# Expert weights in a decoder block: low parts in place, eight load slots instead of six, four high buffers instead of three, and an index column copied one expert ahead

## The chip, the cores and the metric

The kernel runs on one core of one Trainium2 chip. The metric is the device time of one execution in microseconds. The engines are TensorE (PE, with its weight loads as PEld), VectorE (DVE), ScalarE (ACT), GpSimd (POOL) and SyncE (SP), which here issues most of the DMAs.

## The reference, cut to what matters

One hybrid decoder block on 512 tokens of width 1024, all in float32: a token mixer (Mamba-2 scan and causal pooling), then a mixture of 32 experts of which each token takes four, then an embedding gate and a final norm. The change touches the experts only:

```python
gu = xb @ w_gate_up[e] + b_gate_up[e]          # (rows, 1024) @ (1024, 2048)
gate, up = jnp.split(gu, 2, axis=-1)
gate = jnp.minimum(gate, SWIGLU_LIMIT)
up = jnp.clip(up, -SWIGLU_LIMIT, SWIGLU_LIMIT)
act = (up + 1.0) * gate * jax.nn.sigmoid(SWIGLU_ALPHA * gate)
return act @ w_down[e] + b_down[e]             # (rows, 1024) @ (1024, 1024)
```

The rows of an expert are gathered from the normed tokens, and its results are weighted and added to the residual at the same tokens. An expert has 8 MiB of gate and up weights and 4 MiB of down weights, so the 32 experts read 384 MiB.

## The kernel before

The products are made more exact by splitting each operand in two parts. The high part is what a copy to the type float32r keeps, the low part is the operand minus its high part. A product is then high x high + low x high + high x low, three matmuls for one.

The weights come in chunks of 1 MiB, 128 partitions by 2048 numbers, twelve for an expert (`CHUNKS`): eight of gate and up (`UP`), each 128 input rows by 2048 columns, and four of down (`DN`), each two blocks of 128 by 1024. Every chunk goes the same way. SP loads it into one of the six slots of `ring` (`RING`; lines 696 to 709) as soon as the slot's last content has been subtracted, which it sees by `lo_done`. ACT copies it to one of three buffers `split_h` (`SPLIT`; `high`, line 1298), for which it waits for the load (`e_loaded`) and for PE to have used the chunk three before (`chunk_used`). DVE subtracts the copy from the slot into one of three buffers `split_l` (`low`, line 1924), for which it waits for `hi_done`. PE multiplies with the high part after `hi_done` and with the low part after `lo_done`, and then raises `chunk_used`. So after the subtraction the slot is free, and PE needs the two split buffers only.

The chunks form one sequence over all experts: gate-up chunks of expert e+1 stand before the down chunks of expert e, which PE multiplies while ACT and DVE make the activation of expert e+1. `chunk_at(j, e, i)` gives a chunk's number, counted from the loop body of expert e: i from 0 to 7 are gate-up chunks, 8 to 11 down chunks, and 12 onward the next ones.

The experts are sorted by how many rows they have. The fuller ones take up to 96 rows (`ROWS`), with their rows' high and low parts in two tiles, `xgT_h` and `xgT_l`: three groups of four matmuls for each gate-up chunk. The others take at most 64 rows (`HALF`), and then the high parts of the rows stand in the lower half of the columns of `xgT_h` and their low parts in the upper half: two groups for each chunk (`half_gate_up`, `half_down`), after which the two halves of the sum are joined by way of `fold` or `y_fold` (`join_halves`). The two kinds alternate; the loops of PE, ACT, DVE and POOL step over pairs, those of SP over single experts.

Each engine's order is written out by hand. ACT's list for an expert has, between its twelve `high` copies, the gate's silu (`gate`, or `halves_out` and `half_gate`), the high parts of the next rows turned (`turned_high`, line 1292), the y output scaled out of PSUM (`y_out`, `half_down_out`, `half_y_out`), and the activation turned. DVE's list has, between its twelve `low` subtractions, `up` (line 1912: the clipped up part, and the product with the silu, `act_done`) and the low parts of what was turned (`turned_low`, line 1931).

POOL fetches the rows: for each expert it waits until PE has turned the last fetched rows (`et_done`), copies the column of row numbers of the expert three ahead from the table `slots` to `icur`, and issues an indirect DMA from `h_rows` into `xg` (`gather`, line 910, `fetch`, line 903). Then it waits for the expert's y (`y_evac`), copies its column to `dcur`, and issues an indirect DMA that adds `y_sb` to `x1_rows` (`scatter`, line 931); when this has landed it raises `y_free`, for which ACT waits before it writes `y_sb` or `y_fold` again. It also copies each expert's weights to `wcur`.

SP's order is: four DMAs for the bias of the next expert (they wait for `bias_used`), eight gate-up loads, four down loads; before each load stands one wait. `position` reads an expert's number out of the sorted list.

Of the kernel before, what the change touches and what calls it, by code (L numbers as in the profile page):

```python
# [50 lines left out]
RING = 6  # L51
SPLIT = 3
# [134 lines left out]
def program(nc, x, p, mix_norm_g, w_in, conv_w, conv_b, dt_bias, a_log, d_skip, ssd_norm_g,  # L187
# [4 lines left out]
    with ctx:  # L192
# [172 lines left out]
        ring = [here(f"ring{i}", [P, 2 * DM], F32) for i in range(RING)]  # L365
# [9 lines left out]
        split_l = [here(f"split_l{i}", [P, 2 * DM], F32R) for i in range(SPLIT)]  # L375
# [7 lines left out]
        icur = here("icur", [ROWS, 1], I32)  # L383
        dcur = here("dcur", [ROWS, 1], I32)
# [136 lines left out]
        e_loaded = [sem(f"e_loaded{i}") for i in range(RING)]  # L521
# [66 lines left out]

        def chunk_at(j, e, i):

            return j * NE * CHUNKS + e * CHUNKS + UP + i

        def raw_loaded(j, e, i):

            return (j * (NE * CHUNKS // RING) + e * (CHUNKS // RING) + (UP + i) // RING + 1) * 16

# [15 lines left out]
        def _(sp):  # L612
# [91 lines left out]
            def down(j, e, i, of, r):  # L704

                slot = (UP + i) % RING
                sp.wait_ge(lo_done, chunk_at(j, e, i) + 1)
# [11 lines left out]
            def weights(j, ahead=0):  # L719
# [10 lines left out]
                with sp.Fori(1 if ahead else 0, NE - 1) as e:  # L730
                    of, after = (position(sp, e), position(sp, e + 1)) if ahead else (e, e + 1)
                    bias_parts(j * NE + e + 1, after)
                    for k in range(UP):
                        gate_up(j, e, k, after, k)
                    for r in range(DN):
                        down(j, e, UP + r, of, r)
                of = position(sp, NE - 1) if ahead else NE - 1
# [12 lines left out]
            for k in range(RING):  # L750
                gate_up(0, 0, k - UP, 0, k, True)
# [11 lines left out]
            for k in range(RING, UP):  # L763
                gate_up(0, 0, k - UP, 0, k)
# [28 lines left out]
        def _(pool):  # L793
# [109 lines left out]
            def fetch(rows=ROWS):  # L903

                g.indirect_dma_start(out=xg[0:rows, :], out_offset=None, in_=h_rows,  # L905
                                     in_offset=bass.IndirectOffsetOnAxis(ap=icur[0:rows, 0:1], axis=0),
# [24 lines left out]
            def scatter(n, col, steps, following=None, landed=True, rows=ROWS):  # L931
# [16 lines left out]
            def one_pass(j):  # L948
# [36 lines left out]

                if isinstance(j, int):
                    rows_of(0, ROWS, ROWS)
                    with pool.Fori(0, PAIRS - 1) as i:
                        rows_of(i * 2 + 1, HALF, ROWS)
                        rows_of(i * 2 + 2, ROWS, HALF)  # L990
# [34 lines left out]
        def _(act):  # L1025
# [272 lines left out]
            def high(j, e, i):  # L1298

                at, s = chunk_at(j, e, i), UP + i  # L1300
                act.wait_ge(e_loaded[s % RING], raw_loaded(j, e, i))
                act.wait_ge(chunk_used, at + CHUNKS - SPLIT + 1)
                a.activation(split_h[s % SPLIT][:, :], ring[s % RING][:, :], ACT.Copy).then_inc(hi_done, 1)  # L1303
# [44 lines left out]
            def one_pass(j):  # L1348
# [40 lines left out]
                def rest(e, more, rows_in, rows_act, folds=None):  # L1389

                    turned_high(t0 + 3 + e * 2, xgT_h, rows_in, 1.0 if more else 1.0 / ALPHA)
                    for i in range(12, 14):
                        high(j, e, i)
                    if folds is not None:
                        half_down_out(e, e)
                    high(j, e, 14)
                    if folds is None:
                        y_out(j, e, 11, n0 + e)
                    else:
                        half_y_out(e, folds)  # L1400
                    high(j, e, 15)
                    if more:
                        turned_high(t0 + 4 + e * 2, actT_h, rows_act, 1.0 / ALPHA)
                        for i in range(16, 22):
# [1335 lines left out]
```

## Time and profile before

| | us |
|---|---|
| median of 3 runs | 1766.81 |
| lowest and highest | 1766.56, 1767.76 |
| the profiled execution | 1766.66 |
| its span | 1764.9 |

Granted clock of TensorE in that execution: 0.998 of full speed. Busy in the span: PE 1698.8 us (96%), DVE 1381.7 (78%), ACT 1200.8 (68%), POOL 713.1 (40%).

The span is the time from the first to the last instruction of the profiled execution. Engines are shown by how long they worked on instructions; waiting isn't counted. "DMA share" is the mean busy share of the 16 DMA engines, by the time their packets took, and it can pass 1 a little since packets overlap. In an instruction row the bracket tells how long the engine sat idle before it and what ended the wait. "DMA to landing" is the time from issue to the completion of a load. Busy shares of a whole run mix two stages here: the projections and the scan up to about 650 us, the experts from there to about 1690.

### The profile page before, as it was taken

The page shows a single profiled execution, that of the slowest core. Times are in us where ns is not written, and L with a number is a line of the kernel's source. Part 1 is how long each engine was busy: PE and PEld are TensorE (multiplying, and loading weights), DVE is VectorE, ACT ScalarE, POOL GpSimd, SP SyncE. Part 2 cuts the span into 40 slices and gives each one's busy share as a digit, 9 for nine tenths or more (in the row PEclk, how much of TensorE's full clock was granted, in tenths as well). Part 3 has the DMA queues.
Part 4 walks back from the last instruction along what each step waited for, and adds up shares of the span by engine and source line. Part 5 has one row for each costly group of instructions (what it writes and reads, how often), then busy time and mean ns, then how long its engine had stood idle before and what let it go on. Part 6 is the DMA issues. An engine that isn't in the chain of part 4 may idle for free.

```text
span 1764.9 us, 24895 instructions
## 1 busy us (share of the span) xinstructions
PE 1698.8 (96%) x8477; PEld 1346.8 (76%) x8477; DVE 1381.7 (78%) x1048; ACT 1200.8 (68%) x967; POOL 713.1 (40%) x344
## 2 busy tenths in 40 slices
PE   6999999999999999999999999999999999999998
PEld 5878889777888987767767767767767767767776
DVE  4666776755334389999999999999999999999984
ACT  5565555433223368788788788788788788788775
POOL 6124233550000072355465365365365365365110
PEclk9999999999999999999999999999999999999999
DMA  5443343433336469999999999999999999999951
GB/s 177 122 129 85 121 122 107 121 108 119 96 96 231 164 218 397 391 404 392 399 402 392 399 401 392 402 406 388 404 404 391 405 400 398 402 400 395 408 201 49
DMA packets 150865, 504.64 MB, mean 286 GB/s; under 512 B 12733, under 2 KB 73285, under 8 KB 117173
## 3 DMA queue, kind: packets, MB, share of 16 engines
q1 hardware_dynamic: 141652, 478.49, 70.0%
q0 software_dynamic: 9104, 25.28, 6.0%
q8 instruction: 39, 0.64, 0.1%
q14 instruction: 22, 0.17, 0.0%
q10 hardware_dynamic: 48, 0.07, 0.0%
HBM read 487.63 MB, written 20.28 MB: 288 GB/s over the span
## 4 chain that ended last, share of the span: by engine, by line
PE 68%; DVE 14%; issue 9%; ACT 6%; POOL 2%; DVEq 0%; ACTq 0%; POOLq 0%
PE gu_ps L2395 13%; DVE split_l L1928 9%; PE gu_ps L2147 8%; PE gu_ps L2149 8%; PE gu_ps L2148 8%; PE dn_ps L2453 7%; PE gu_ps L2399 7%; PE dn_ps L2459 3%; ACT split_h L1303 3%; PE gu_ps L2409 2%; PE dn_ps L2652 1%; PE gu_ps L2652 1%; PE et_ps L2381 1%; DVE up_sb L1915 1%; PE gu_ps L2169 1%
## 5 line engine op out<-in xcount | busy, mean ns | idle before, releaser
L1928 DVE TENSOR_TENSOR split_l<-ring,split_h 128x2048 fp32r<-128x2048 f32 x384 | 864.8, 2285 | 71.0 <-ACT split_h L1303 69.3
L1303 ACT ACTIVATE split_h<-ring 128x2048 fp32r<-128x2048 f32 x384 | 729.9, 1913 | 113.8 <-PE gu_ps L2399 62.7
L914 POOL COPY icur<-slots 96x1 int32 x30 | 282.8, 9428 | 412.3 <-PE et_ps L2381 410.1
L1536 DVE TENSOR_TENSOR w_lo<-w_raw,w_hi 128x2048 fp32r<-128x2048 f32 (+1 forms) x45 | 104.3, 2318 | 128.8 <-ACT w_hi L1035 122.6
L2409 PE MATMUL gu_ps<-split_l,xgT_h 128*128 128x512 f32 x480 | 139.6, 412 | 17.8 <-DVE split_l L1928 14.0
L2147 PE MATMUL gu_ps<-hT_h,w_hi 128*128 128x512 f32 x392 | 154.6, 394 | 0.6 <-DVE acc L1589 0.6
L2149 PE MATMUL gu_ps<-hT_h,w_lo 128*128 128x512 f32 x392 | 152.7, 390 | 0.0
L2148 PE MATMUL gu_ps<-hT_l,w_hi 128*128 128x512 f32 x392 | 152.6, 389 | 0.0
L2395 PE MATMUL gu_ps<-split_h,xgT_h 128*128 128x512 f32 x512 | 140.6, 396 | 0.9 <-DVE xgT_l L1934 0.9
L2399 PE MATMUL gu_ps<-split_l,xgT_h 128*128 128x512 f32 x512 | 137.2, 390 | 0.0
L2395 PE MATMUL gu_ps<-split_h,xgT_l 128*128 128x512 f32 x512 | 137.2, 390 | 0.0
L2409 PE MATMUL gu_ps<-split_h,xgT_h 128*128 128x512 f32 x480 | 134.4, 402 | 0.0
L2409 PEld LDWEIGHTS gu_ps<-split_l,xgT_h 128*128 128x128 f32 x480 | 83.2, 188 | 64.2 <-DVE split_l L1928 50.7
L1035 ACT ACTIVATE w_hi<-w_raw 128x2048 fp32r<-128x2048 f32 (+1 forms) x45 | 85.0, 1889 | 56.8 <-PE gu_ps L2149 51.4
L923 POOL DMA_INDIRECT slot_rows<-routed,row_idx x16 | 28.2, 1763 | 232.8 <-DVE row_idx L1849 228.3
L2399 PEld LDWEIGHTS gu_ps<-split_l,xgT_h 128*128 128x128 f32 x512 | 96.1, 188 | 20.6
L2395 PEld LDWEIGHTS gu_ps<-split_h,xgT_l 128*128 128x128 f32 x512 | 96.1, 188 | 20.5
L2395 PEld LDWEIGHTS gu_ps<-split_h,xgT_h 128*128 128x128 f32 x512 | 93.7, 188 | 22.3 <-issue 3.4
L2409 PEld LDWEIGHTS gu_ps<-split_h,xgT_h 128*128 128x128 f32 x480 | 86.7, 188 | 26.4 <-issue 9.2
L938 POOL DMA_INDIRECT x_rows<-y_sb,dcur x31 | 91.2, 2942 | 27.6 <-POOL dcur L935 27.6
L905 POOL DMA_INDIRECT xg<-h_rows,icur x31 | 79.8, 2573 | 26.6 <-POOL icur L914 26.3
L2147 PEld LDWEIGHTS gu_ps<-hT_h,w_hi 128*128 128x128 f32 x392 | 73.6, 188 | 16.8 <-issue 1.6
(426 smaller groups left out, 3242.1 us busy)
## 6 DMA issues: line engine op xcount, KB each, us to landing
ring<-in_w_gate_up SPq DMA_DIRECT2D x256, 1024.0 KB, 8.0
ring<-in_w_down SPq DMA_DIRECT2D x128, 1024.0 KB, 9.2
w_raw<-in_w_in SPq DMA_DIRECT2D x28, 1024.0 KB, 5.9
arow<-acum_rows POOLq DMA_DIRECT2D x16, 512.0 KB, 6.5
w_raw<-in_w_ssd_out SPq DMA_DIRECT2D x8, 1024.0 KB, 5.4
w_raw<-in_w_in SPq DMA_DIRECT2D x9, 512.0 KB, 6.1
w_raw<-in_w_mix_out SPq DMA_DIRECT2D x4, 1024.0 KB, 7.9
wpg<-in_w_ple_gate SPq DMA_DIRECT2D x2, 2048.0 KB, 19.9
```

What stands on the lines that cost most here:

```text
L914: g.tensor_copy(icur[:, :], col).then_inc(idx_done, 1)
L938: g.indirect_dma_start(out=x1_rows, out_offset=bass.IndirectOffsetOnAxis(ap=dcur[0:rows, 0:1], axis=0), in_=y_sb[0:rows, :], in_offset=Non ...
L1303: a.activation(split_h[s % SPLIT][:, :], ring[s % RING][:, :], ACT.Copy).then_inc(hi_done, 1)
L1536: v.tensor_tensor(w_lo[RAW_SLOT[n]][:, 0:size], w_raw[RAW_SLOT[n]][:, 0:size], w_hi[HI_SLOT[n]][:, 0:size].bitcast(F32), ALU.subtract).the ...
L1928: v.tensor_tensor(split_l[s % SPLIT][:, :], ring[s % RING][:, :], split_h[s % SPLIT][:, :].bitcast(F32), ALU.subtract).then_inc(lo_done, 1)
L2147: o = t.matmul(pb(key)[:, cols], sh, mh, start=n == 0, stop=False)
L2148: o = t.matmul(pb(key)[:, cols], sh, ml, start=False, stop=False)
L2149: o = t.matmul(pb(key)[:, cols], sl, mh, start=False, stop=n == len(parts) - 1)
L2395: t.matmul(gu_ps[:, b * 512:b * 512 + 512], x[:, k, :], split_h[s][:, b * 512:b * 512 + 512], start=False, stop=False)
L2399: o = t.matmul(gu_ps[:, b * 512:b * 512 + 512], xgT_h[:, k, :], split_l[s][:, b * 512:b * 512 + 512], start=False, stop=k == KD - 1)
L2409: o = t.matmul(gu_ps[:, b * 512:b * 512 + 512], xgT_h[:, k, :], part[s][:, b * 512:b * 512 + 512], start=False, stop=False)
L2453: t.matmul(ps[:, b * 512:b * 512 + 512], x[:, 2 * r + k, :], split_h[s][:, k * DM + b * 512:k * DM + b * 512 + 512], start=r == 0 and k == ...
```

## The change

The low part is written over the slot that it is computed from: `ring_low` are tiles at the addresses of `ring`, and `split_l` is gone. Its three buffers' room goes to two more slots, of the eight that there are now, and to a fourth high buffer. SP may reload a slot when PE has used the chunk in it (`chunk_used`) instead of when it has been subtracted. Since twelve chunks aren't a multiple of eight slots, the loops of SP, ACT, DVE and PE go by pairs of experts, and the slot is found from the place in the pair (`slot_of`). The two new slots use load semaphores that had one use before, hence `before` in `raw_loaded`.

In ACT's list one more `high` stands before the gate, before the turned rows, before the y output and before the turned activation; in DVE's list one more `low` stands before `up`, before the turned rows and before the turned activation.

POOL copies the index column of the rows that it will fetch for the next expert right behind a fetch, into `icur` and `icur_odd` by turns, so that a fetch follows `et_done` at once; and it copies `dcur` before it waits for y.

The diff, cut to its core (the fallback for more than 96 rows, and lines that only hand over the new arguments, are left out):

```diff
-RING = 6
-SPLIT = 3
+RING = 8
+FIRST = 6
+SPLIT = 4
...
-        ring = [here(f"ring{i}", [P, 2 * DM], F32) for i in range(RING)]
+        ring_off = top[0]
+        ring = [here(f"ring{i}", [P, 2 * DM], F32) for i in range(FIRST)]
+        top[0] = ring_off
+        ring_low = [here(f"ring_low{i}", [P, 2 * DM], F32R) for i in range(FIRST)]
...
-        split_l = [here(f"split_l{i}", [P, 2 * DM], F32R) for i in range(SPLIT)]
+        ring_off = top[0]
+        ring += [here(f"ring{i}", [P, 2 * DM], F32) for i in range(FIRST, RING)]
+        top[0] = ring_off
+        ring_low += [here(f"ring_low{i}", [P, 2 * DM], F32R) for i in range(FIRST, RING)]
...
-        e_loaded = [sem(f"e_loaded{i}") for i in range(RING)]
+        e_loaded = [sem(f"e_loaded{i}") for i in range(FIRST)] + yT_loaded[0:RING - FIRST]
...
+        def slot_of(e, i):
+
+            return (in_pair(e)[1] * CHUNKS + UP + i) % RING
...
             def gate_up(j, e, i, of, k, first=False):
 
-                slot = (UP + i) % RING
+                slot = slot_of(e, i)
                 if not first:
-                    sp.wait_ge(lo_done, chunk_at(j, e, i) + 1)
+                    sp.wait_ge(chunk_used, chunk_at(j, e, i) + CHUNKS - RING + 1)
...
-            for k in range(RING, UP):
-                gate_up(0, 0, k - UP, 0, k)
+            for k in range(FIRST, UP):
+                gate_up(0, 0, k - UP, 0, k, True)
...
-                pool.wait_ge(y_evac, n + 2)
-                alone(pool)
-                g.tensor_copy(dcur[:, :], col).then_inc(idx_done, 1)
+                if index_first:
+                    g.tensor_copy(dcur[:, :], col).then_inc(idx_done, 1)
+                pool.wait_ge(y_evac, n + 2)
+                alone(pool)
+                if not index_first:
+                    g.tensor_copy(dcur[:, :], col).then_inc(idx_done, 1)
...
+                def rows_ahead(e, rows_in, rows_out, index, other, more=True):
+
+                    pool.wait_ge(et_done, t0 + e * 2 + 4)
+                    alone(pool)
+                    pool.wait_ge(idx_done, k0 + e * 2 + 4)
+                    alone(pool)
+                    fetch(rows_in, index)
+                    if more:
+                        index_of(e + 4, other)
+                    scatter(e, slots[0:ROWS, column(e), 0], k0 + e * 2 + (6 if more else 5),
+                            slots[0:ROWS, column(e + 1), 1].bitcast(F32), True, rows_out, True)
...
-                act.wait_ge(e_loaded[s % RING], raw_loaded(j, e, i))
+                act.wait_ge(e_loaded[slot_of(e, i)], raw_loaded(j, e, i))
                 act.wait_ge(chunk_used, at + CHUNKS - SPLIT + 1)
...
                 def expert(e, more, rows_in=ROWS, folds=None):
 
-                    gate(j, e, UP - 1, n0 + e + 1)
                     high(j, e, 10)
+                    gate(j, e, UP - 1, n0 + number(e) + 1)
                     high(j, e, 11)
...
                 def half_expert(e, folds):
 
-                    halves_out(e, e + 1)
                     high(j, e, 10)
+                    halves_out(e, number(e) + 1)
+                    high(j, e, 11)
                     half_gate(folds)
-                    high(j, e, 11)
...
-                v.tensor_tensor(split_l[s % SPLIT][:, :], ring[s % RING][:, :], split_h[s % SPLIT][:, :].bitcast(F32),
-                                ALU.subtract).then_inc(lo_done, 1)
+                v.tensor_tensor(ring_low[slot_of(e, i)][:, :], ring[slot_of(e, i)][:, :],
+                                split_h[s % SPLIT][:, :].bitcast(F32), ALU.subtract).then_inc(lo_done, 1)
...
                 def expert(e, more, half_next=False):
 
-                    up(ROWS, chunk_used, chunk_at(j, e, UP - 1) + CHUNKS + 1, n0 + e + 1)
                     low(j, e, 10)
+                    up(ROWS, chunk_used, chunk_at(j, e, UP - 1) + CHUNKS + 1, n0 + number(e) + 1)
                     low(j, e, 11)
```

## Rows read from the trace of the kernel before

**Rows 1.** The page: DMA's busy tenths in 40 slices; the costliest group.

```profile
DMA  5443343433336469999999999999999999999951
...
L1928 DVE TENSOR_TENSOR split_l<-ring,split_h 128x2048 fp32r<-128x2048 f32 x384 | 864.8, 2285 | 71.0 <-ACT split_h L1303 69.3
```

**Rows 2.** The chain that ended last: start us, us, what; two of its pieces.

```profile
1083.61 2.29 DVE split_l L1928
...
1149.40 2.29 DVE split_l L1928
```

**Rows 3.** Busy time by stretch: loads ahead of the experts, clean, after a scatter, one pair.

```profile
core 0: us, PE busy (x) PEld busy (x) DVE busy (x) ACT busy (x) POOL busy (x), PEclk, DMA share, GB/s
570.00:575.00 5.00, 5.00 (x44) 5.00 (x44) 1.91 (x4) 0.00 (x0) 0.00 (x0) 1.00 1.02 431
575.00:580.00 5.00, 5.00 (x45) 5.00 (x44) 0.84 (x2) 2.44 (x4) 0.00 (x0) 1.00 1.01 421
...
1116.45:1119.74 3.29, 3.29 (x16) 2.73 (x15) 3.29 (x3) 2.87 (x2) 3.29 (x1) 1.00 1.03 436
1132.90:1136.19 3.29, 3.29 (x17) 2.71 (x16) 2.86 (x2) 2.49 (x2) 1.15 (x2) 1.00 1.02 354
1136.19:1139.48 3.29, 3.29 (x16) 2.74 (x15) 2.84 (x2) 2.49 (x2) 0.00 (x0) 1.00 1.05 331
1149.10:1214.90 65.80, 63.63 (x292) 47.66 (x292) 61.28 (x33) 54.54 (x35) 35.32 (x11) 1.00 1.02 400
```

**Rows 4.** Timeline of DVE and PE where a half expert begins: start us, us, instruction.

```profile
1142.60 2.29 DVE L1928 TENSOR_TENSOR split_l<-ring,split_h 128x2048 fp32r<-128x2048 f32 x1 [0.43 <-ACT split_h L1303]
...
1144.81 1.22 DVE L1915 TENSOR_SCALAR up_sb<-gu_ps 96x1024 f32<-96x1024 f32 x1
...
1149.54 0.76 PEld L2430 LDWEIGHTS dn_ps<-split_l,actT_h 128*128 128x128 f32 x4 [1.40 <-DVE split_l L1928]
```

**Rows 5.** Waits of the whole run: who for whom, total us, times, longest.

```profile
PEld gu_ps L2409 <- DVE split_l L1928: 50.7, 88, 1.4
...
PEld dn_ps L2430 <- DVE split_l L1928: 28.1, 30, 1.5
...
ACT split_h L1303 <- DMA ring<-in_w_down: 7.3, 11, 1.2
```

**Rows 6.** Weight loads: two single ones by line, then all 24 of a pair.

```profile
L702 SPq DMA_DIRECT2D ring<-in_w_gate_up x1: 332/332/332, 1149.6 to 1149.6; - x1
...
DMA to landing us min/median/max: 6.7/6.7/6.7
...
L702 SPq DMA_DIRECT2D ring<-in_w_gate_up x1: 333/333/333, 1151.8 to 1151.8; - x1
...
DMA to landing us min/median/max: 6.9/6.9/6.9
...
DMA to landing us min/median/max: 6.7/8.9/10.8
```

**Rows 7.** Timeline of DVE in the router: not in place, then in place.

```profile
616.12 0.29 DVE L1816 TENSOR_TENSOR oh<-erow,ixf 128x128 f32<-128x128 f32 x1
...
618.73 0.29 DVE L1860 TENSOR_TENSOR oh<-oh,routed 128x128 f32<-128x128 f32 x1
```

**Rows 8.** Timeline of POOL, and DVE and ACT beside it, in one pair.

```profile
1115.73 9.74 POOL L914 COPY icur<-slots 96x1 int32 x1 [12.39 <-PE et_ps L2381]
...
1118.75 9.08 DVE L1928 TENSOR_TENSOR split_l<-ring,split_h 128x2048 fp32r<-128x2048 f32 x4
...
1129.81 3.24 POOL L938 DMA_INDIRECT x_rows<-y_sb,dcur  x1 [0.90 <-POOL dcur L935]
...
1148.60 10.34 POOL L914 COPY icur<-slots 96x1 int32 x1 [14.54 <-PE et_ps L2381]
...
1153.38 1.02 ACT L1321 ACTIVATE y_fold<-dn_ps 64x1024 fp32r<-64x1024 f32 x1 [0.69 <-PE dn_ps L2419]
...
1159.33 2.29 DVE L1928 TENSOR_TENSOR split_l<-ring,split_h 128x2048 fp32r<-128x2048 f32 x1 [0.44 <-ACT split_h L1303]
```

More of the change, by code:

```diff
@@ L584, in conv_tile, with in_pair, number @@
             return {"X": 4 * g + (key[2] if len(key) > 2 else 0), "B": 16 + g, "C": 20 + g}[key[0]]
+        def in_pair(e):
+            return (0, e) if isinstance(e, int) else e
+        def number(e):
+            return e if isinstance(e, int) else e[0] * 2 + e[1]
         def chunk_at(j, e, i):
-            return j * NE * CHUNKS + e * CHUNKS + UP + i
+            pair, off = in_pair(e)
+            return j * NE * CHUNKS + pair * (2 * CHUNKS) + off * CHUNKS + UP + i
+        def slot_of(e, i):
+            return (in_pair(e)[1] * CHUNKS + UP + i) % RING
         def raw_loaded(j, e, i):
-            return (j * (NE * CHUNKS // RING) + e * (CHUNKS // RING) + (UP + i) // RING + 1) * 16
+            pair, off = in_pair(e)
+            before = 1 if slot_of(e, i) >= FIRST else 0
+            return (j * (NE * CHUNKS // RING) + pair * (2 * CHUNKS // RING) + (off * CHUNKS + UP + i) // RING + 1 + before) * 16
         def passes(eng):
@@ L729, in weights, with expert_loads @@
                     sp.wait_ge(order_done, 1)
-                with sp.Fori(1 if ahead else 0, NE - 1) as e:
-                    of, after = (position(sp, e), position(sp, e + 1)) if ahead else (e, e + 1)
-                    bias_parts(j * NE + e + 1, after)
+                def expert_loads(e):
+                    n = number(e)
+                    of, after = (position(sp, n), position(sp, n + 1)) if ahead else (n, n + 1)
+                    bias_parts(j * NE + n + 1, after)
                     for k in range(UP):
@@ L736, in weights @@
                         down(j, e, UP + r, of, r)
+                with sp.Fori(0, PAIRS) as i:
+                    for off in (1, 2) if ahead else (0, 1):
+                        expert_loads((i, off))
+                if not ahead:
+                    expert_loads(NE - 2)
                 of = position(sp, NE - 1) if ahead else NE - 1
@@ L748, in weights @@
                 alone(sp)
-            for k in range(RING):
+            for k in range(FIRST):
                 gate_up(0, 0, k - UP, 0, k, True)
@@ L2423, in half_down @@
             def half_down(e, r):
-                at, s = chunk_at(0, e, UP + r), (2 * UP + r) % SPLIT
-                for part, ready, count in ((split_h, hi_done, at + 1), (split_l, lo_done, at + RING + 1)):
+                at, high_part, low_part = chunk_at(0, e, UP + r), split_h[(2 * UP + r) % SPLIT], ring_low[slot_of(e, UP + r)]
+                for part, ready, count in ((high_part, hi_done, at + 1), (low_part, lo_done, at + RING + 1)):
                     pe.wait_ge(ready, count)
@@ L2498, in expert @@
                     if r == 2 and more:
-                        rows_in(t0 + 1, j * NE + e + 2)
+                        rows_in(t0 + 1, j * NE + number(e) + 2)
                     elif r == 2:
```

135 lines of the change are left out of this document (74 added, 61 removed).

## The prediction

> **What bounds the kernel now.** I read the slices of the page first. They show two stages: up to about 650 us the input projections, then until about 1690 us the experts, in which the DMA engines are busy at nine tenths or more in every slice [rows 1]. The change touches nothing before the first expert load, so only the second stage can move. The chain of waits gives its beat: the same subtraction returns at 1083.61 and 1149.40, so a pair of experts (one full, one half) takes 65.8 us, and there are some 15 such pairs [rows 2].
>
> Inside a pair the busy times by stretch come next [rows 3]: of 65.8 us PE is busy 63.6, DVE 61.3, ACT 54.5, and the DMA share is 1.02. The timeline says how the engines hand over [rows 4]. In the full expert's gate-up PE sets the pace and DVE idles 0.43 us ahead of each subtraction, because ACT may be only three high buffers ahead. Then the half expert begins: DVE has the subtractions plus `up` and the product, PE needs fewer matmuls for each chunk, and PE waits, 1.40 us at 1149.54. Over the run PE's weight loads wait 50.7 + 28.1 = 78.8 us for low parts [rows 5], 5.3 us a pair. ACT waits for a load only 7.3 us in all, 0.5 us a pair [rows 5]. So in this view the compute loop is the bound, and one more chunk of lead is worth something.
>
> But the DMA rows say that there is hardly anything to feed a faster loop with. A pair needs 24 loads of 1 MiB, 25.2 MB; the pair's row has 400 GB/s, 26.3 MB. The load issued at 1149.6 takes 6.7 us, the next, at 1151.8, takes 6.9 [rows 6]: they land at 1156.3 and 1158.7, 2.4 us apart, which is one load at 436 GB/s, the best stretch there is [rows 3]. These are the shortest waits of that pair; landings there are always behind another load. I read both as: compute is the bound by its waits, and DMA is within a few per cent of being the bound as well.
>
> **The change part by part.** Time is counted against the profiled execution: span 1764.9, its own time 1766.66, practically the median 1766.81. 15 pairs carry the sum.
>
> *Low parts in place.* A subtraction keeps its shape. In place and not in place stand side by side in the router: 0.29 us and 0.29 us for 128x128 [rows 7]. I take zero. Bounds: their rounding, 0.01 us in 0.29, is 3.5%, or 0.08 us on each of 24 subtractions of 2.285 us [rows 1]: -2 to +2 us a pair of DVE time, and DVE has 65.8 - 61.3 = 4.5 us to spare, so even the bad end is covered as long as DVE isn't made the bound.
>
> *Slots.* Before, a slot was reloaded when its subtraction had ended; now when PE has used it, but two slots later. The load of chunk c left at low(c-6), and low runs one to two chunks ahead of PE's end, so about 7 to 7.5 chunks ahead of use. Now it is 8. Loads leave up to one chunk earlier, and never later by this count. SP's wait is on a later event, but what is queued behind it is only the next loads and the four bias DMAs, which stay ahead of their chunk. At the start chunks 6 and 7 no longer wait; ACT wasn't waiting for them. Zero.
>
> *Four high buffers, and ACT's and DVE's order.* ACT may be one more chunk ahead, and each rearranged list puts one copy or subtraction before the gate, the turned rows and the y output instead of after. Because the lead is one chunk more, these fall where they fell: low(10) takes the place of low(9) at 1142.60, `up` stays at 1144.81 [rows 4]. PE then finds one more low part ready when the half expert begins: one subtraction, 2.3 us, off its 5.3 us of waits. If DVE also fills all of its idle time, a pair is 61.3. So the compute loop alone would come to 65.8 - 2.3 = 63.5, at best 61.3; the next thing late would be DVE itself.
>
> *What DMA allows.* Loads at the best rate, 24 x 2.4 = 57.7 us. The other 1.1 MB at the same rate, 2.6. After each scatter the rate falls to 354 and 331 for 6.6 us [rows 3]: (431 - 343) / 431 x 6.6 = 1.35 us, twice a pair, 2.7. Together 63.0 us: the floor. With six loads queued at once ahead of the experts the rows have 431 and 421 in two stretches of 5 us [rows 3]; at 426 the loads are 59.1 and a pair 64.4. The other end is that the share of 1.02 means what it says, no DMA engine ever rests, and a pair stays at 65.8. The nearest rows for a deeply queued stream are those of the six loads, but they have no gathers among them; so I take the middle of 64.4 and 65.8, 65.05. Gain 0.75 x 15 = 11 us: 1766.7 - 11 = 1756. The rest of the compute gain is not had: what is late next is a load, and ACT's waits for `ring` should grow where its waits for PE shrink.
>
> The Trainium skill (DMA: Bandwidth & Descriptors, Where 436 GB/s comes from) puts a ceiling of about 435 GB/s on what the 16 engines move into SBUF. The best rows agree (436 in 3.3 us). By that figure alone 26.3 MB are 60.5 us, as an estimate, 5 us under the present pair; it leaves out what the scatters cost.
>
> *GpSimd.* Before, one expert's chain is: wait for the turned rows, index copy (9.74 us at 1115.73), gather, `dcur`, scatter at 1129.81 [rows 8]. The copy now runs behind the gather, so the gather leaves about 10 us earlier, and the copy is in front of the scatter: 1115 + 1 + 2.4 + 9.7 + 1 = 1129, the same place. PE doesn't wait for gathered rows now, so the earlier gather is worth nothing by itself. The number of copies is the same but for one. Queued behind the copy are `dcur`, the scatter and `y_free`, on which ACT's next y copy waits (at 1153.38 [rows 8]). The scatter's slow stretch ends at about 1141, so this has some 12 us of cover. Zero; without the cover, a microsecond for each microsecond.
>
> *Loops by pairs.* SP, ACT, DVE and PE step through the same number of instructions; SP reads the order twice an expert as before. Zero.
>
> **The rivals.**
>
> *DMA has nothing left.* A server that never rests can't be sped up by queueing more. For it: 1.02 in the pair's row, and latencies that never fall to that of a lone load. Against it: the pairs repeat to 0.05 us and no wait for a load lies on the chain, and if DMA alone set the beat ACT would be waiting for it. Time: 1766.7 less at most 3 us at the drain: 1763.5 to 1768, no change.
>
> *DMA gives way entirely.* Its rate may follow the demand, the 1.02 being an artefact of overlapping packets. Then the compute loop gets its 2.3 to 4.5 us a pair: 1766.7 - 35 to 68, 1699 to 1732. Against it is the floor of 63.0 worked out above, which already forbids more than 2.8 us a pair (1725).
>
> *Slower: GpSimd is kept out.* The two index copies of a pair take 9.74 and 10.34 us though they write 96 numbers; the second ends at 1158.94, just as DVE pauses, 0.44 us before 1159.33 [rows 8]. They seem to be held by DVE's back-to-back subtractions, and the change removes DVE's pauses. The copy now stands in front of the scatter. It decides from the point where a copy lasts 10 + 12 = 22 us: then `y_free` is late, ACT stops at the y copy and all high parts behind it. At 25 us that is 3 us a pair, 45 us, 1812. Against it: the copy of 1115.73 ended at 1125.5 in the middle of four subtractions without a pause [rows 8], so a boundary between two is enough. The Trainium skill (SBUF — State Buffer, SBUF: two separate sides) has the rule behind this: a DVE instruction with two SBUF inputs and a GpSimd instruction that reads SBUF exclude each other for the whole instruction.
>
> **How the numbers follow.** DMA binds after a small gain, 1744 to 1763: 0.47, likeliest, 1756. DMA has nothing left: 0.28. DMA gives way: 0.13. GpSimd kept out: 0.08, and 0.04 for an in-place subtraction at or beyond its bad end. A measurement of this kernel tells about 0.2%, 3.5 us, from no change. Faster 0.47 + 0.13 = 0.60, same 0.28, slower 0.12. The range takes in the first two cases and the upper half of the third: 1722 to 1769, 0.81.
>
> **What would show it.** Pairs of 65.0 us; ACT's waits for `ring` loads at 1 to 3 us a pair instead of 0.5; time to landing up from a median of 8.9 [rows 6] to 11 or more, since freed slots wait in DMA's queue; PE's waits for low parts down from 5.3 us. The rate in the pair's row should be 404 GB/s. If it stays at 400 with landings longer, the first rival holds; if it passes 415, the second. Index copies of over 20 us and ACT waiting for `y_free` would be the third. I am wrong at the root if ACT's waits for loads don't grow at all.

## The result and the profile after

The changed kernel takes 1776.46 us (median of five runs, 1775.26 to 1780.36) where the kernel before takes 1766.81: a ratio of 1.0058, with an interval of 1.0046 to 1.0070. It is slower by 9.7 us, and outside the range of the prediction. The profiled execution of after has 1776.46 us too, with a span of 1774.7.

The page of the changed kernel: span, DMA's tenths, the chain by engine, three groups (busy us, mean ns, idle before and releaser), and the weight loads (median us to landing).

```profile
span 1774.7 us, 24821 instructions
...
DMA  5443434333336369999999999999999999999941
...
PE 68%; DVE 9%; issue 8%; DMA 7%; ACT 5%; POOL 2%; DVEq 0%; ACTq 0%; SPq 0%; POOLq 0%
...
L1985 DVE TENSOR_TENSOR ring_low<-ring,split_h 128x2048 fp32r<-128x2048 f32 x384 | 862.1, 2284 | 56.7 <-ACT split_h L1357 55.0
L1357 ACT ACTIVATE split_h<-ring 128x2048 fp32r<-128x2048 f32 x384 | 727.9, 1913 | 127.0 <-PE gu_ps L2459 51.7
L937 POOL DMA_INDIRECT xg<-h_rows,icur_odd x15 | 200.0, 13334 | 277.1 <-PE et_ps L2441 277.1
...
ring<-in_w_gate_up SPq DMA_DIRECT2D x256, 1024.0 KB, 10.2
ring<-in_w_down SPq DMA_DIRECT2D x128, 1024.0 KB, 10.7
```

The subtraction in place takes 2284 ns, against 2285 [rows 1]. The loads now land after 10.2 and 10.7 us (medians; 8.0 and 9.2 before). And DMA stands on the chain with 7%, all of it `down` loads.

The waits of the changed kernel (who for whom, total us, times, longest):

```profile
ACT split_h L1357 <- DMA ring<-in_w_down: 48.1, 40, 2.4
...
PE gu_ps L2502 <- ACT fold L1369: 32.6, 15, 3.5
...
PEld gu_ps L2469 <- DVE ring_low L1985: 20.9, 43, 0.5
...
PEld dn_ps L2490 <- DVE ring_low L1985: 0.3, 1, 0.3
```

PE's waits for low parts fell from 50.7 to 20.9 us (L2469, the old L2409) and from 28.1 to 0.3 (L2490, the old L2430) [rows 5]: 78.8 us have become 21.2. In their place ACT waits 48.1 us for `down` loads, 3.2 us a pair instead of 0.5 (and 2.8 us in all for gate-up loads), and PE waits 32.6 us where the two halves are joined.

Two pairs by stretch (us, busy and count of PE, PEld, DVE, ACT and POOL, then PEclk, DMA share, GB/s), to lay beside the 65.80 us of [rows 3]; then one slice out of the first:

```profile
1043.00:1109.59 66.59, 64.01 (x292) 49.24 (x292) 61.34 (x32) 54.42 (x34) 38.02 (x10) 0.97 1.01 391
1109.59:1175.94 66.35, 62.62 (x293) 48.06 (x292) 61.29 (x32) 54.78 (x34) 41.62 (x12) 1.00 1.02 398
...
1046.33:1049.66 3.33, 3.33 (x9) 2.63 (x10) 2.76 (x3) 3.30 (x3) 0.00 (x0) 0.53 1.02 353
```

The pairs no longer repeat to the hundredth. By the starts of `fold`, the first two are 65.06 and 64.96 (714.97 to 780.02 to 844.98), the other twelve lie between 65.4 and 66.8 and average 66.35; below I call them pairs of 66.3. From the first `fold` to the last, 14 pairs, the changed kernel needs 926.2 us and the kernel before 920.9. That is 5.3 us of the loss. Another 2.3 us are lost ahead of the first `fold` (where ACT waits 3.9 us for `down` loads, before 1.2) and 2.2 us behind the last.

ACT's timeline at the end of the second pair (start us, us, instruction, idle before it), and the two loads behind its waits:

```profile
1167.42 1.92 ACT L1357 ACTIVATE split_h<-ring 128x2048 fp32r<-128x2048 f32 x1 [0.55 <-PE gu_ps L2469]
1171.56 1.91 ACT L1357 ACTIVATE split_h<-ring 128x2048 fp32r<-128x2048 f32 x1 [2.21 <-DMA ring<-in_w_down]
1174.00 1.92 ACT L1357 ACTIVATE split_h<-ring 128x2048 fp32r<-128x2048 f32 x1 [0.53 <-DMA ring<-in_w_down]
1175.94 1.87 ACT L1369 ACTIVATE fold<-gu_ps 64x2048 fp32r<-64x2048 f32 x1
```

```profile
L732 SPq DMA_DIRECT2D ring<-in_w_down x1: 383/383/383, 1156.6 to 1156.6; - x1
...
DMA to landing us min/median/max: 10.7/10.7/10.7
...
L732 SPq DMA_DIRECT2D ring<-in_w_down x1: 384/384/384, 1159.2 to 1159.2; - x1
...
DMA to landing us min/median/max: 12.2/12.2/12.2
```

These two land at 1156.6 + 10.7 = 1167.3 and 1159.2 + 12.2 = 1171.4, 4.1 us apart where the usual distance is 2.4 to 2.5, and ACT starts on each 0.1 us after it has landed. The `fold`, and with it PE's join, come late by what ACT lost.

### The profile page after: what moved, and what is told of

Its sections match the earlier page's. It is cut to its first block, busy times and chain, and to the rows that moved or that the text cites. A ratio compares the mean times of both kernels' runs of the same rounds, so it can differ in the third digit from the quotient of the medians.

```text
span 1774.7 us, 24821 instructions
## 1 busy us (share of the span) xinstructions
PE 1696.1 (96%) x8477; PEld 1362.6 (77%) x8477; DVE 1379.4 (78%) x1048; ACT 1198.8 (68%) x967; POOL 801.4 (45%) x344
## 4 chain that ended last, share of the span: by engine, by line
PE 68%; DVE 9%; issue 8%; DMA 7%; ACT 5%; POOL 2%; DVEq 0%; ACTq 0%; SPq 0%; POOLq 0%
PE gu_ps L2455 13%; PE gu_ps L2207 8%; PE gu_ps L2209 8%; PE gu_ps L2208 8%; DMA ring<-in_w_down 7%; PE gu_ps L2459 7%; PE dn_ps L2513 6%; PE gu_ps L2469 4%; DVE ring_low L1985 4%; PE dn_ps L2519 3%; PE et_ps L2441 2%; ACT fold L1369 2%; PE dn_ps L2713 1%; PE gu_ps L2713 1%; PE gu_ps L2229 1%
## 5 line engine op out<-in xcount | busy, mean ns | idle before, releaser
L1985 DVE TENSOR_TENSOR ring_low<-ring,split_h 128x2048 fp32r<-128x2048 f32 x384 | 862.1, 2284 | 56.7 <-ACT split_h L1357 55.0
L937 POOL DMA_INDIRECT xg<-h_rows,icur_odd x15 | 200.0, 13334 | 277.1 <-PE et_ps L2441 277.1
L2469 PE MATMUL gu_ps<-split_h,xgT_h 128*128 128x512 f32 x480 | 134.0, 401 | 7.5 <-DVE xgT_h L1991 7.5
L2459 PE MATMUL gu_ps<-ring_low,xgT_h 128*128 128x512 f32 x512 | 137.2, 390 | 0.0
L2469 PE MATMUL gu_ps<-ring_low,xgT_h 128*128 128x512 f32 x480 | 134.2, 401 | 2.9
L955 POOL DMA_INDIRECT slot_rows<-routed,row_idx x16 | 28.2, 1763 | 232.9 <-DVE row_idx L1906 228.3
L1023 POOL COPY icur<-slots 96x1 int32 x14 | 131.8, 9415 | 0.0
L937 POOL DMA_INDIRECT xg<-h_rows,icur x16 | 73.8, 4614 | 92.9 <-PE et_ps L2441 52.2
L2469 PEld LDWEIGHTS gu_ps<-ring_low,xgT_h 128*128 128x128 f32 x480 | 86.7, 188 | 37.5 <-DVE ring_low L1985 20.9
L2469 PEld LDWEIGHTS gu_ps<-split_h,xgT_h 128*128 128x128 f32 x480 | 86.7, 188 | 34.1 <-DVE xgT_h L1991 11.6
L2459 PEld LDWEIGHTS gu_ps<-ring_low,xgT_h 128*128 128x128 f32 x512 | 96.1, 188 | 20.6
L909 POOL TENSOR_TENSOR dx<-xs_tok,dsk 128x512 f32<-128x512 f32 x16 | 19.0, 1188 | 156.7 <-DVE zs L1762 156.6
## 6 DMA issues: line engine op xcount, KB each, us to landing
ring<-in_w_gate_up SPq DMA_DIRECT2D x256, 1024.0 KB, 10.2
ring<-in_w_down SPq DMA_DIRECT2D x128, 1024.0 KB, 10.7
```

What stands on the lines that cost most here:

```text
L1023: g.tensor_copy(index[:, :], slots[0:ROWS, column(e), 0]).then_inc(idx_done, 1)
L1985: v.tensor_tensor(ring_low[slot_of(e, i)][:, :], ring[slot_of(e, i)][:, :], split_h[s % SPLIT][:, :].bitcast(F32), ALU.subtract).then_inc( ...
L2459: o = t.matmul(gu_ps[:, b * 512:b * 512 + 512], xgT_h[:, k, :], low_part[:, b * 512:b * 512 + 512], start=False, stop=k == KD - 1)
L2469: o = t.matmul(gu_ps[:, b * 512:b * 512 + 512], xgT_h[:, k, :], part[:, b * 512:b * 512 + 512], start=False, stop=False)
```

## The experiments

Theory A: the loads. DMA was full already, and is the bound of the changed loop. Theory B: the new lists; `fold` stands behind a high part that waits for a load. Theory C: GpSimd is held by DVE. (In the expectations A is also called D, B is F or L, and C is G or H.) Later the first split in two: the amount of DMA work, or the room, in chunks, between the release of a slot and the moment ACT wants its next content. The chips differ: the kernel before takes 1775.8 to 1775.9 us beside `a_half_order`, the three runs with another GpSimd order, those with two rows and those with light matmuls, and 1767.0 to 1767.2 beside the others. Every ratio is against the kernel before on the same chip.

### The order of the half expert, and of GpSimd

```diff
 a_half_order: ACT, half_expert
-                    high(j, e, 10)
                     halves_out(e, number(e) + 1)
-                    high(j, e, 11)
+                    high(j, e, 10)
                     half_gate(folds)
+                    high(j, e, 11)
 a_pool_old: POOL, for every expert
-                        rows_ahead(i * 2 + 1, HALF, ROWS, icur, icur_odd)
+                        rows_of(i * 2 + 1, HALF, ROWS)
```

> The changed kernel with ACT's order in the half expert as before: fold, high(10), silu of the gate, high(11). Theory F (fold order): in the changed kernel the fold stands behind a high copy that waits for a load, PE stalls at the join (32.6 us in all), releases no slots meanwhile, and its clock falls. Then this kernel loses the join stalls, the clock stays at 1.00, a pair is 65.0 to 65.5 us instead of 66.3, and the time is 1758 to 1766. Theory G (GpSimd): what costs is that gathers and scatters take longer on the DMA engines in their new places. Then the join stall goes but ACT waits for loads elsewhere, a pair stays at 66 or more: 1773 to 1778.

Measured: 1786.04, ratio 1.0058 (1.0041 to 1.0075). The wait at the join fell from 32.6 to 14.1 us, and ACT's waits for loads rose from 48.1 + 2.8 to 41.7 + 28.2 (`down` + gate-up). The lateness only moved; B loses.

> The changed kernel with GpSimd's order as before: index copy, gather, then the copy for the scatter behind the wait for y. Theory F: nothing changes, the fold is still behind the load, 1774 to 1779. Theory G: the gather is issued in 2.4 us again and not in 13, the rate after the scatters doesn't fall to 280 GB/s, a pair is 65.0 to 65.8: 1756 to 1767.

Measured: 1860.48, ratio 1.0474 (1.0457 to 1.0492). Its waits and, below them, PE's timeline:

```profile
PEld et_ps L2438 <- DMA xg<-h_rows,icur: 97.7, 14, 7.3
...
1085.08 1.54 PE L2438 MATMUL et_ps<-ident,xg 96*128 96x96 f32 x8 [6.41 <-DMA xg<-h_rows,icur]
```

With the copy ahead of the gather, in the changed loop, the gathered rows come 6 to 7 us late in every pair; the gather takes 7.4 us on GpSimd by itself (mean). Neither theory had foreseen that. So the new order of GpSimd isn't decoration: the rest of the change needs it.

> The changed kernel with both orders as before, so slots, in-place low parts and the fourth high buffer remain. If F and G each hold in part, this is the fastest of the four, 1750 to 1762. If the DMA engines alone set the pair's time whatever the orders, it is 1766 or more, and ACT's waits for loads take the place of the rest.

Both edits together: four runs from 1804.31 to 1832.25, ratio 1.0235 (1.0148 to 1.0322, the widest interval here), with 52.7 us of waits for gathered rows. The wait for rows remains. ACT's old order, which changed nothing by itself, takes off half of the loss here; the two edits are not additive, why isn't shown, and I draw no more from it.

> The kernel before with nothing but GpSimd's new order. Theory F: 1766 to 1768, no change. Theory G: slower by 3 to 10 us, since DMA has no slack, with ACT waiting for loads by 20 us or more in all where it waited 7.3.

The kernel before with the new GpSimd order alone (`rows_ahead` and `icur_odd`): 1776.90, ratio 1.0009 (1.0000 to 1.0019). ACT's waits for `down` loads go from 7.3 to 22.1 us, as C said, but the time hardly moves: the pairs average 65.95 us (65.1 to 67.3). GpSimd's order by itself costs about a microsecond, by the interval 3.4 us at most.

### The lists, the fourth buffer, the slots

> The changed kernel once more, so that the three beside it are compared on one chip. Slower than the kernel before by 0.4 to 0.8%, with pairs of 66.3 us, as in its first runs.

The changed kernel once more, on the chip of the runs that follow: 1778.22, ratio 1.0075 (1.0057 to 1.0092).

```diff
 a_orders_old: ACT's and DVE's lists as before (one of the places)
-                    high(j, e, 10)
                     gate(j, e, UP - 1, n0 + number(e) + 1)
+                    high(j, e, 10)
 a_split3
-SPLIT = 4
+SPLIT = 3
 a_ring6
-RING = 8
+RING = 6
```

> The changed kernel (eight slots, low parts in place, four high buffers, GpSimd's new order) with ACT's and DVE's lists as before, so that no copy or subtraction stands ahead of the gate, the turned rows or the y output where it stood behind them. Theory H (starved GpSimd): DVE running without a pause keeps GpSimd from making its descriptors; the lists don't change how long DVE runs, so the time stays at 0.4 to 0.8% over the kernel before. Theory L (lists): a copy that waits for a load now holds up the fold, the gate and the turned rows; with the old lists the pair falls to 65.8 or less and the time is that of the kernel before or up to 0.6% better.

Measured: 1777.94, ratio 1.0070 (1.0053 to 1.0086), ACT waiting 38.3 + 31.9 us for loads. The lists make no difference; again only the place of the lateness changes. The run settles another rival too. The changed kernel's granted clock is 0.99 over the run, here it is 0.998 as in the kernel before, and the time is the same: the loss doesn't come from a lower clock.

> The changed kernel with three high buffers used instead of four. ACT and DVE can be three chunks ahead of PE, no more, as before. Theory H: DVE has its short pauses in the full gate-up and ahead of the half expert again, GpSimd's gathers are issued in 3 to 5 us instead of 13, and the time falls by 0.3 to 0.6%. Theory D (DMA bound whatever the lead): no change against the changed kernel within 0.2%. If the lists are written for four buffers, it may also be slower by 0.5% or more, through PE waiting for low parts.

Measured: 1830.21, ratio 1.0356 (1.0338 to 1.0373). Among its waits there is none for a load; PE waits for low parts instead:

```profile
PEld dn_ps L2490 <- DVE ring_low L1985: 31.6, 14, 2.3
PEld gu_ps L2469 <- DVE ring_low L1985: 26.7, 46, 1.4
```

> The changed kernel with six slots in use, released by PE. This is what the in-place low parts cost if no slots are given back: a load leaves six chunks ahead of PE's use instead of 7 to 7.5. Theory D and my count of slots: ACT waits for loads for 100 us or more in all and the time is 3 to 8% over the kernel before. If DMA only needs one load queued to be fully busy, it is under 1.5%.

Measured: 1873.63, ratio 1.0610 (1.0593 to 1.0628):

```profile
ACT split_h L1357 <- DMA ring<-in_w_gate_up: 104.5, 93, 2.6
...
ACT split_h L1357 <- DMA ring<-in_w_down: 80.2, 94, 2.5
```

Working in place without the two extra slots costs 6%. Read with `a_split3` this gave the idea of the room, the lead that a load has over the high part that wants it. A slot is released when PE has used chunk c-8, and with four high buffers ACT may want chunk c when PE has used c-4: four chunks. With six slots it is two; with eight slots and three high buffers it is five, and then no load is waited for. That `a_split3` is slower all the same may lie in lists written for four buffers; three buffers with the old lists weren't run.

### What the loop does with less DMA

```diff
 a_gather2 and a_two_rows: the gathers of the loop
-                    fetch(rows_in, index)
+                    fetch(2, index)
 a_scatter2 and a_two_rows: the scatters
-IndirectOffsetOnAxis(ap=dcur[0:rows, 0:1], axis=0), in_=y_sb[0:rows, :]
+IndirectOffsetOnAxis(ap=dcur[0:2, 0:1], axis=0), in_=y_sb[0:2, :]
 b_half_load: each expert load
-                sp.dma_start(ring[slot][:, :], src)
+                sp.dma_start(ring[slot][:, 0:wide], src[:, 0:wide])
```

`wide` is half of the columns; the `down` loads are halved in the same way.

> The changed kernel with every gather and every scatter inside the expert loop cut to two rows, so most rows that an expert works on are stale and most of its results aren't added; the weights, the matmuls and the splits are all there. It takes the row traffic, about 1.1 MB a pair and the slow stretches behind it, off the DMA engines. Theory D (DMA sets the changed kernel's pair of 66.3 us: 24 loads at 2.48 us, 59.5, and 6 to 7.5 for the rows): a pair falls to 61.5 to 63.5, where DVE and PE bind, so 1766 - 40 to 70 = 1700 to 1735, and ACT's waits for loads shrink below 20 us. Theory H (the compute engines and GpSimd bind through their own waits): 1765 or more.

Measured: 1746.49, ratio 0.9829 (0.9813 to 0.9846). A is borne out in the main; the pair stops just above the 61.5 to 63.5 us that I expected.

> The kernel before with the same cut to two rows (stale rows, results mostly not added). If its compute loop alone makes the 65.8 us, as its chain of waits says, the time stays within 0.3% of 1767. If DMA makes them, it falls by 15 us or more.

Measured: 1775.74, ratio 0.9997 (0.9987 to 1.0007). The pair by stretch, of the changed kernel with few rows and of the kernel before with few rows:

```profile
782.60:846.40 63.80, 62.65 (x293) 47.99 (x294) 60.62 (x33) 53.66 (x34) 44.71 (x11) 1.00 0.99 402
```

```profile
1000.00:1065.80 65.80, 63.51 (x294) 47.68 (x293) 61.25 (x33) 54.55 (x35) 34.92 (x11) 1.00 0.98 385
```

This is the cleanest pair of runs of the study. The changed compute loop is a loop of 63.8 us, the old one of 65.8; with the row DMAs gone only the new one gains.

> The kernel before with each expert load cut to half its bytes (half of every slot keeps old content, so half of the weights are left out); subtractions, copies and matmuls keep their sizes. DMA is then free. If the compute loop alone sets the pair of 65.8 us before the change, this is 1764 to 1768 (or faster only at the start and end of the loop, where loads are waited for). If the full DMA queues were part of the 65.8 us, a pair falls below 65 us and the kernel below 1755.

Measured: 1766.77, ratio 0.9999 (0.9990 to 1.0009), with the same chain, to the hundredth, as [rows 2], though only half of the bytes move:

```profile
1083.61 2.29 DVE split_l L1929
...
1149.40 2.29 DVE split_l L1929
```

```profile
1083.61:1149.40 65.79, 63.48 (x292) 47.67 (x292) 61.28 (x34) 54.53 (x35) 35.33 (x11) 1.00 0.67 207
```

The 65.8 us of before are compute's alone. The full DMA queues beside it had no part in them.

> The changed kernel with only the gathers of the expert loop cut to two rows; the scatters stay whole, and nearly all gathered rows are left out. With both kinds of row DMA cut a pair lasted 63.8 us and the kernel 1746; with both whole 66.3 and 1776. If the gathers take most of the DMA time that binds the pair, this gives 1748 to 1756. If the scatters take most of it, 1765 to 1774. If it is only bytes, both kinds are about 0.57 MB a pair each, so half of the 30 us: about 1761.

> The changed kernel with only the scatters of the expert loop cut to two rows; the gathers stay whole, and nearly all rows of y are left out of the sum. The complement of the run with the gathers cut. The slices of 280 to 354 GB/s stand behind scatters, so I expect more of the 30 us here: 1750 to 1756, pairs of 64 to 64.5 us. Were it the gathers, whose issue GpSimd drags over 10 to 14 us, this would be 1765 to 1774.

Measured, on the quicker chip: 1738.39 with the gathers cut, ratio 0.9843 (0.9826 to 0.9859); 1741.47 with the scatters cut, 0.9854 (0.9838 to 0.9871). The pair, gathers cut, then scatters cut:

```profile
1028.20:1091.92 63.72, 62.58 (x293) 48.02 (x293) 60.54 (x33) 53.64 (x34) 44.85 (x11) 1.00 1.01 407
```

```profile
1030.93:1094.71 63.78, 62.62 (x293) 47.97 (x293) 60.60 (x33) 53.73 (x34) 44.85 (x11) 1.00 1.01 404
```

All three forms of my expectation missed: either kind alone gives back the whole loss and the whole gain. The pair falls to the compute loop's 63.8 and stops there. So each kind is worth at least 66.3 - 63.8 = 2.5 us of a pair of the changed kernel, and the 24 loads with one kind still beside them fit into 63.8.

Theory C goes with them. With the scatters cut the gathers are whole, GpSimd needs longer to issue them than in the changed kernel (13.7 us against 13.3, the fifteen of `icur_odd`), and the pair is still 63.8:

```profile
L937 POOL DMA_INDIRECT xg<-h_rows,icur_odd x15 | 205.7, 13713 | 260.1 <-PE et_ps L2441 260.1
...
ACT y_sb L1393 <- POOL wcur L961: 60.3, 14, 4.4
```

The second row is the mechanism of my third rival, at another place: in 14 pairs ACT waits over 4 us for a copy of expert weights that GpSimd finishes late (3 times, 11.9 us in all, in the changed kernel; never in the kernel before). It is covered. In a pair of `a_gather2`, which has the same 14 waits, the chain runs past it on PE.

### The room

```diff
 a_lead7, and with the gathers cut too a_lead7_gather2
-                sp.wait_ge(chunk_used, chunk_at(j, e, i) + CHUNKS - RING + 1)
+                sp.wait_ge(chunk_used, chunk_at(j, e, i) + CHUNKS - RING + 2)
 b_late1
-                sp.wait_ge(lo_done, chunk_at(j, e, i) + 1)
+                sp.wait_ge(lo_done, chunk_at(j, e, i) + 2)
```

> The changed kernel, but each load waits for PE's use of the chunk seven before instead of eight, so one load less stands in the DMA queues. If the depth of the load queue makes the row DMAs dearer (they share the 16 engines with four to six loads instead of three to four) a pair falls back to 65.8 us or below and the kernel to 1767 or less. If the DMA work of a pair is the same whatever the depth, and it alone sets 66.3 us, this is the same as the changed kernel, 1774 to 1779. If loads come too late at the scatters, ACT waits more for loads and it is slower, 1785 or more.

Measured: 1828.26, ratio 1.0336 (1.0318 to 1.0354).

> The changed kernel with both edits that were made singly: each load waits for the chunk seven before instead of eight, and the gathers of the expert loop are cut to two rows (nearly all gathered rows are left out). Singly the first gave 1828 and the second 1738. If a pair of the changed kernel is set by the DMA work alone, the work is now below the compute loop's 63.8 us and this stays at 1738 to 1745. If the room between a slot's release and the moment ACT wants the next chunk counts by itself, three chunks are too few with any amount of work, and this is 1765 or more.

Measured: 1799.18, ratio 1.0181 (1.0164 to 1.0198).

> The kernel before, with each load waiting for one more subtraction than the slot needs, so it leaves one chunk later; nothing else changes. The room from a load's issue to the moment ACT may want it falls from about 4.25 chunks to 3.25. If before has DMA slack in its pair of 65.8 us, a later start costs little: 1767 to 1775. If before too lives from that room, as the changed kernel does (four chunks: 1776, three: 1828), this is 1800 to 1830.

Measured: 1831.63, ratio 1.0368 (1.0331 to 1.0404). A pair of each, in this order:

```profile
997.40:1067.26 69.86, 64.39 (x292) 48.91 (x292) 61.91 (x32) 55.10 (x34) 26.90 (x10) 0.98 0.98 377
```

```profile
1052.08:1120.28 68.20, 64.11 (x292) 49.11 (x292) 61.55 (x32) 54.88 (x34) 26.54 (x10) 0.97 0.97 373
```

```profile
1064.40:1133.17 68.77, 64.29 (x296) 47.88 (x294) 61.37 (x32) 54.93 (x35) 38.38 (x10) 1.00 1.00 383
```

One chunk of room less costs about 50 us in the changed kernel, 61 us in it with the gathers cut (1738 to 1799), and 64 us in the kernel before. The rate falls to 373 to 383 GB/s. DMA must have rested in between, since it had moved the same bytes in 65.8 us, though its share is 0.97 to 1.00. Nor is it the clock: it is 1.00 in the last of the three pairs.

In time, the room is what lies between a load's issue and the start of its high part. Matching the first load with the first high part, the second with the second and so on, for the loads issued between 850 and 1600 us, gives the last two columns (means of 245 to 284 loads, in us; of 198 in the third row, where some landings are missing):

| kernel | room, chunks | ACT waits for loads, us | ratio | room | landing |
|---|---|---|---|---|---|
| changed, six slots | 2 | 184.7 | 1.061 | 8.6 | 7.8 |
| changed, a chunk late | 3 | 75.1 | 1.034 | 10.6 | 8.9 |
| the same, gathers cut | 3 | 53.8 | 1.018 | 10.1 | 8.5 |
| changed | 4 | 50.9 | 1.006 to 1.008 | 12.2 | 10.9 |
| the same, old lists | 4 | 70.2 | 1.007 | 14.3 | 13.0 |
| changed, gathers cut | 4 | 6.3 | 0.984 | 11.4 | 8.4 |
| changed, three high buffers | 5 | none listed | 1.036, by low parts | 14.5 | 7.7 |
| before, a chunk late | 3 to 4 | 78.9 | 1.037 | 9.4 | 7.7 |
| before | 4 to 5 | 7.3 | 1 | 11.2 | 8.5 |

The room in us did not shrink from the kernel before to the changed one. What grew is the time to landing, by 2.4 us, and with it 55 of the 270 high parts start within 0.15 us of a landing, where it was 10 of 273. And more room alone doesn't help the changed kernel: its old lists give 2 us more, the landings grow by as much, and the time is the same. In both of these no load was issued with fewer than two earlier ones still on the way. That holds for the kernel before as well, so DMA was near its limit there already; but a load has 2.5 others ahead of it there on average and 3.4 in the changed kernel, and the shortest landing is 6.2 against 7.3 us (4.6 with the scatters cut). In the kernels with a chunk less, some loads leave with one ahead of them or none.

### Two that told little

Leaving out the matmuls with the rows' low parts in full experts was meant to uncover DMA's own pace.

```diff
-for x in (xgT_h, xgT_l):
+for x in (xgT_h,):
```

> The changed kernel without the low x high matmuls of the full experts, a third of their matmuls, so PE needs about 11 us less a pair and the products are less exact. All the loads, copies, subtractions and row DMAs stay. If DMA sets the pair, it stays at 66 us and more (time 1770 to 1780, apart from a few us in the first and last expert); if the compute loop does, it falls towards DVE's 62 us, 1715.

> The kernel before with the same matmuls left out. With PE out of the way this measures what its DMA and DVE allow with six slots: if DMA had the slack that I forecast, a pair is 64 to 65.3 us and the time 1740 to 1760. If DMA was full already, it stays within 0.3% of 1767.

Measured: 1794.58, ratio 1.0104 (1.0078 to 1.0129), and 1787.72, 1.0067 (1.0043 to 1.0090). Both became slower with less work. The changed one has GpSimd's gathers through `icur` at 15.6 us (mean), and PE waiting 62.2 us for their rows; its granted clock in the loop is 0.92 of full speed (0.95 in the other). With matmuls, gathers and clock changed at once they don't separate anything, though neither shows a DMA that had speed in reserve.

## Why the prediction was wrong

*What bounds the kernel before: right.* Compute by its waits; half the DMA bytes changed nothing.

*The compute loop: right.* Predicted 63.5 us, measured 63.8. PE's waits for low parts fell as said.

*In place: right.* 2284 ns against 2285. *The new lists:* zero, right.

*What DMA allows: the step that failed.* I took the middle of 64.4 and 65.8 (it is 65.1, not 65.05, which changes nothing). The low end was 59.1 for the loads and 5.3 for the rest. The loads' term was right. Away from long gaps landings follow each other by 2.46 us in both kernels (mean of those under 2.62 us), and 24 x 2.46 = 59.0. The rest was mis-sized: 66.3 - 59.0 is 7.3 us, 2 us more than I had. The gathers stood in it with their bytes alone, about half of the 2.6 us, since I gave the slow stretches to the scatters; the runs with one kind cut show at least 2.5 us for each kind. How the rest of the 2 us is divided isn't shown. The high end was worse founded. 65.8 was no measure of DMA but of compute, as `b_half_load` shows, and I took it as the longest pair that could come. In the changed loop, with two or more earlier loads always on the way, a pair took 66.3. A middle between a low guess and the present time could only come out as a gain.

*Slots: zero.* For the step from before to after that was right: the room went from 11.2 to 12.2 us, and is 11.4 where the changed loop runs at its own pace. By count, loads leave up to a chunk earlier, and the fourth high buffer lets ACT ask a chunk earlier as well. What I didn't see is that landings grow when a faster loop has more loads queued (3.4 ahead of each instead of 2.5, 10.9 us instead of 8.5), so that loads come too late for the faster asker. That wasn't among my rivals. The "1 to 3 us a pair" of waits for loads that I forecast (3.2 came) were in the text, but I had booked them as ending a gain, not as a loss.

*GpSimd: zero, right for the scatter, wrong in the reason for the gather.* I wrote that the earlier gather was worth nothing. `a_pool_old` shows that without it the changed kernel would be 4.7% slower than the kernel before: the cost is hidden by the very edit that I held worthless. The third rival's mechanism is there too (copies and gathers of 9 to 14 us, and the late copy of expert weights), but ACT never waited for `y_free`, and `a_scatter2` has more of it and is faster.

*The first rival* (nothing left in DMA, 1763.5 to 1768) was nearest to what happened, but assumed that a full server stays at its 65.8, so its range ended at no change.

*Rate and landing.* I forecast 404 GB/s and a landing of 11 us or more; 391 to 398 and 10.2 to 10.7 came, and I had said that 400 with longer landings means the first rival. That test pointed the right way.

What stays open: why the DMA work that fitted into 65.8 us takes 66.3. The difference sits in the long gaps between landings: 28 of 4 to 5 us in the changed kernel, 12 in the kernel before, of some 270 each. Less row DMA makes the changed kernel faster, and less room makes both kernels slower; that is shown. What lengthens the gaps isn't. Gathers that GpSimd issues slowly are hardly the cause, since `b_pool_new` has gathers of 11 us and pairs of 65.95. The 2.2 us behind the last `fold` weren't followed up. A ninth slot would need room on the chip that I didn't find, and wasn't tried. No version that computes the whole result beat the kernel before.

## What to carry to other kernels

Count a load's room at both ends: from the release of its buffer to the first moment that the next engine may ask for it. Buffers added behind the ring take from this room, slots added to it give; where it was short, one chunk was worth 50 to 64 us here. Then set it against the time to landing in the loop that you forecast, not in the one that you have: that time grew from 8.5 to 10.9 us, and 2 us more of room gained nothing. A busy share of DMA near 1 measures no need. Find the need by cutting bytes, of each kind of DMA by itself, before a gain is forecast from a faster loop (the kernel before at half the load bytes: no change; the changed kernel without one kind of row DMA: 2% faster than itself).

## What the runs showed of the hardware

The DMA share isn't proportional to bytes. It is 1.02 at 400 GB/s, 0.98 at 385, 0.99 at 402 and 0.67 at 207. The last moves half the bytes of the first with two thirds of the share. So it can't tell how much slack there is.

GpSimd's instructions stretch while DVE subtracts without a pause. POOL's timeline in the changed kernel; DVE runs from 1149.2 to 1172.7 without a break:

```profile
1120.96 9.76 POOL L937 DMA_INDIRECT xg<-h_rows,icur  x1 [7.53 <-issue]
1130.72 0.20 POOL L1023 COPY icur_odd<-slots 96x1 int32 x1
...
1150.20 13.73 POOL L937 DMA_INDIRECT xg<-h_rows,icur_odd  x1 [14.54 <-PE et_ps L2441]
1163.93 8.84 POOL L1023 COPY icur<-slots 96x1 int32 x1
```

The same copy takes 0.20 us where DVE has a gap of 0.57 us and 8.84 beside the subtractions; the gather's issue takes 13.73. For the copy, that agrees with the rule of the Trainium skill (SBUF — State Buffer, SBUF: two separate sides), that a DVE instruction with two SBUF inputs and a GpSimd instruction that reads SBUF exclude each other. The boundary between two subtractions, which I had held to be enough for GpSimd, isn't always.

TensorE's granted clock is 0.53 in the slice at 1046.33 shown above, so nearly all of it at the lower level of 1.2 GHz. Shortly before, PE had stood 2.85 us at the join; in the next slice the clock is 1.00, the level of 2.4 GHz:

```profile
1045.02 1.11 PE L2502 MATMUL gu_ps<-fold,shift 64*64 64x512 f32 x4 [2.85 <-ACT fold L1369]
```

```profile
1049.66:1052.99 3.33, 3.33 (x21) 2.80 (x20) 3.33 (x2) 1.64 (x2) 0.70 (x1) 1.00 0.91 349
```

PE had not lost its clock in the pairs of before, where its longest wait in [rows 5] is 1.5 us.
